# Gate columns in pairs by seven products of halves, w_pg scaled once, and the stages around them re-interleaved

## The chip, the cores and the metric

The kernel runs on all 8 cores of one Trainium2 chip, each with its own share of the batch and no traffic between cores. The metric is the device time of the slowest core, in microseconds (us). The engines are TensorE (PE in the rows), VectorE (DVE), ScalarE (ACT), GpSimd (POOL) and SyncE (SP); the last two issue most of the DMA transfers.

## The reference

One layer of a convolutional decoder trunk and a final norm, on 8 prompt sequences of 2048 tokens and 128 sample sequences of 8 tokens, width 1024. Per core that is one prompt sequence and 16 sample sequences: 2176 tokens.

```python
u = rmsnorm(h, g_mix)
proj = u @ w_in                        # (tokens, 9 * 1024)
a_b, a_c, a_h, a_z, b_v, b_g, b_z, gate_a, gate_b = split(proj)
s  = a_c * a_h                         # branch A
ya = (a_b * causal_dwconv(s, w_conv_a) * silu(a_z)) @ w_out_a          # 3 taps
v  = b_v * sigmoid(b_g)                # branch B
c  = causal_dwconv(v, w_conv_b) + b_conv_b                             # 31 taps
yb = (silu(layernorm(c, ln_g, ln_b)) * silu(b_z)) @ w_out_b
m  = sigmoid(gate_a) * ya + sigmoid(gate_b) * yb
h  = h + m @ w_o
h  = h + sigmoid(rmsnorm(h, g_ple) @ w_pg) * (p @ w_pe)
y  = rmsnorm(h, g_final)               # and the last rows of s and v, per sequence
```

## The kernel before

**Tiles.** A core's tokens go through in two blocks. Block 0 has 1152 tokens (9 tiles of 128) in two units of 2 x 288 tokens, block 1 has 1024 tokens (8 tiles) in one unit of 2 x 512. The normed, transposed input uT stays in SBUF as eight k tiles. Every projection is computed in chunks j = 0 to 7 of 128 output channels: weights of a chunk (128 x 1024, bf16) stay in the array's side and tokens stream, in `mm8` (L582), so a chunk of one column group takes 2 units x 2 halves x 8 k tiles = 32 products of 288 columns in block 0 and 16 of 512 in block 1.

**Weights.** 14 ring buffers of 256 KB are filled by GpSimd's queue (L394) in the order in which they are used (`WL`); a buffer that is done with lets the next transfer be issued.

**Order.** All operations are recorded by `S.add` in program order with what they read and write; an engine works in that order, and waits (semaphores) come from overlaps of reads and writes. There is no planner: the order in the code is the order on each engine. A block runs: the GLU projection, the 31-tap convolution (`s2_conv`, L720, on TensorE from re-laid-out copies R and Rs of prompt and sample rows, which SyncE loads at L687 and L694 from DRAM) and the short convolution chunk by chunk; then conv 6, gate and output product 0 of branch a (`s5_a`), conv 7, `s5_a(1)`, `ln_stats`, `s5_a(2)`, the z branch with LayerNorm applied (`s4_chunk`, z_j) mixed with `s5_a(3)` and `s5_a(4)`, `s5_a(5)` to `s5_a(7)`, and eight `s5_b` in the order 7, 0, 1, ... 6. Then the last stage, per tile: product with w_o (L1004), the residual (VectorE L1015) and its bf16 copy (ScalarE L1020), a transpose by DMA (L1024), products with w_pe (L1052) and w_pg (L1060), and the final norm and output. In block 0 the next block's first stage (statistics, `s1_scale`, transposes) is interleaved with that.

**Around the convolutions.** VectorE evacuates a convolution (L744, L748, a shuffle L751) and adds it and its square into accs and accq (L767, L771), in two parts each. `ln_stats` sums those over partitions by products with ones (L782), makes mean and variance (ScalarE L790, L792, VectorE L794), Ln and Exp (L797, L799), and sends both to DRAM and back, broadcast, into accs and accq (SyncE L803, L809). z's units wait for these (VectorE L923, L925), and ScalarE applies two silus (L918 on z, L927 on the norm).

**Gates.** `s5_half` runs a gate's chunk (columns 7 or 8 of w_in), its Tanh on ScalarE (L938), the output product of the same chunk and an evacuation on VectorE that multiplies with the gate (L946); branch b adds both (L977).

**w_pg.** In the b stage of each block SyncE loads w_pg in f32 (`wpg_stage`, L516, 512 KB a transfer, two staging buffers), ScalarE scales it with g_ple into bf16 (`wpg_scale`, L520, eight times a block).

## Time and profile before

| | |
|---|---|
| median of 3 runs (range) | 862.86 us (861.85 to 863.13) |
| span of the profiled execution (core 4) | 861.8 us |
| spans of the eight cores | 855.7 (core 3) to 861.8 us |
| mean granted clock of the cores | 0.995 to 0.998 |
| TensorE busy | 837.3 us, 97% |
| VectorE busy | 478.1 us, 55% |
| ScalarE busy | 304.0 us, 35% |
| GpSimd busy | 216.1 us, 25% |
| chain that ended last | TensorE 86%, DMA 4%, VectorE 4%, ScalarE 3% |
| 16 DMA engines, 258 to 300 us | 93% busy, 161 GB/s |

The profiled execution's span is 1.06 us under the median of the runs. A row of a timeline has a start, a length, engine, line, operation, output and inputs, and in brackets how long the engine had been idle and what it had waited for. Matmul ends are modelled, so the pace of TensorE is read from start to start. A granted clock of 1 is 2.4 GHz; 0.5 is 1.2 GHz.

### The profile page before, as it was taken

The numbers are of one execution on the slowest core, as the hardware profiler recorded it, in microseconds if no ns is written. First come the engines' busy times: TensorE is split into PE (matmuls) and PEld (weight loads), VectorE is DVE, ScalarE is ACT, GpSimd is POOL, SyncE is SP. The second block draws the span as 40 slices with busy tenths as digits, with TensorE's granted clock in tenths as the row PEclk, the third lists the DMA queues.
The fourth block names the chain that finished last, engine by engine and source line by source line (L and its number), as shares of the span: only waits on it lengthen the run. The fifth ranks groups of instructions, "written<-read, shape, count | busy, mean of one in ns | idle before, by whom it ended". The sixth has DMA issues, their size and how long they took to land.

```text
span 861.8 us, 16560 instructions; the slowest of 8 cores (855.7 to 861.8 us)
## 1 busy us (share of the span) xinstructions
PE 837.3 (97%) x5746; PEld 498.3 (58%) x5790; DVE 478.1 (55%) x676; ACT 304.0 (35%) x426; POOL 216.1 (25%) x402
## 2 busy tenths in 40 slices
PE   7899999999999999999899999999999999999995
PEld 3677777777777777775344444444444444444442
DVE  3545576766856742344776244555566483234566
ACT  3212232322344531434565212222224342242554
POOL 3532332332312111122442222222221221000121
PEclk9999999999999999999999999999999999999998
DMA  9999999999969864799998998998987899353533
GB/s 242 163 195 184 198 157 162 162 170 162 153 100 208 117 98 74 161 232 152 220 274 213 157 154 124 148 146 130 147 140 121 171 167 168 52 159 61 142 100 108
DMA packets 88826, 133.44 MB, mean 155 GB/s; under 512 B 37272, under 2 KB 45736, under 8 KB 86696
## 3 DMA queue, kind: packets, MB, share of 16 engines
q0 software_dynamic: 33392, 57.72, 44.7%
q1 hardware_dynamic: 55208, 74.40, 39.6%
q8 instruction: 47, 0.77, 0.4%
q14 instruction: 35, 0.29, 0.1%
q10 hardware_dynamic: 144, 0.26, 0.1%
HBM read 169.26 MB, written 17.25 MB: 216 GB/s over the span
## 4 chain that ended last, share of the span: by engine, by line
PE 86%; DMA 4%; DVE 4%; ACT 3%; issue 2%; SPq 0%; POOL 0%; DVEq 0%; POOLq 0%; ACTq 0%
PE ps L582 72%; PE ps L1060 5%; PE ps L1004 5%; PE ps L720 3%; DMA t_xs<-x 2%; PE ps L1052 1%; DMA t_ring<-w_in 1%; ACT t_tmp L414 1%; DVE t_cbuf L1015 1%; ACT t_tmp L738 1%; DMA t_u2T<-t_xb 1%; ACT t_cbuf L1074 1%; DVE t_tmp L861 0%; ACT t_xb L1020 0%; DVE t_uT L559 0%
## 5 line engine op out<-in xcount | busy, mean ns | idle before, releaser
L582 PE MATMUL ps<-t_uT,t_ring 128*128 128x288 bf16 (+1 forms) x3429 | 536.9, 316 | 6.0 <-DVE t_uT L559 2.2
L582 PEld LDWEIGHTS ps<-t_uT,t_ring 128*128 128x128 bf16 x3456 | 336.1, 98 | 200.5 <-issue 10.2
L394 POOL DMA_DIRECT2D t_ring<-w_in x144 | 79.1, 550 | 300.5 <-PE ps L582 279.1
L938 ACT ACTIVATE t_tmp<-ps 128x576 f32<-128x576 f32 (+1 forms) x48 | 36.7, 771 | 107.5 <-PE ps L582 107.5
L946 DVE SCALAR_TENSOR_TENSOR t_tmp<-t_tmp,ps 128x576 f32<-128x576 f32 (+1 forms) x27 | 24.6, 910 | 86.1 <-PE ps L582 86.1
L1060 PE MATMUL ps<-t_reg,t_u2T 128*128 128x512 bf16 x267 | 62.7, 386 | 3.4 <-DMA t_u2T<-t_xb 2.6
L582 PE MATMUL ps<-t_yaT,t_ring 128*128 128x288 bf16 (+1 forms) x383 | 61.7, 317 | 0.1
L582 PE MATMUL ps<-t_cbuf,t_ring 128*128 128x288 bf16 (+1 forms) x382 | 61.5, 317 | 0.1
L1004 PE MATMUL ps<-t_cbuf,t_yaT 128*128 128x512 bf16 x267 | 60.7, 379 | 0.3
L905 DVE TENSOR_TENSOR t_tmp<-ps,t_tmp 128x576 f32<-128x576 f32 (+1 forms) x24 | 21.8, 912 | 60.0 <-PE ps L582 60.0
L644 DVE SCALAR_TENSOR_TENSOR t_vta<-t_tmp,ps 128x512 bf16<-128x512 f32 (+1 forms) x24 | 20.7, 863 | 58.2 <-ACT t_tmp L641 50.7
L414 ACT ACTIVATE t_tmp<-t_cbuf 128x1024 bf16<-128x1024 f32 x37 | 38.8, 1049 | 39.0 <-DVE t_cbuf L1085 37.3
L641 ACT ACTIVATE t_tmp<-ps 128x576 f32<-128x576 f32 (+1 forms) x24 | 18.6, 775 | 91.1 <-PE ps L582 91.1
L582 PEld LDWEIGHTS ps<-t_yaT,t_ring 128*128 128x128 bf16 x384 | 37.4, 98 | 21.9 <-issue 0.6
L582 PEld LDWEIGHTS ps<-t_cbuf,t_ring 128*128 128x128 bf16 x384 | 37.6, 98 | 21.4
L1060 PEld LDWEIGHTS ps<-t_reg,t_u2T 128*128 128x128 bf16 x272 | 26.7, 99 | 37.3 <-issue 7.4
L417 POOL TENSOR_SCALAR t_msq<-t_ssq 128x1 f32<-128x1 f32 x50 | 15.9, 319 | 122.3 <-ACT t_tmp L414 121.9
L1004 PEld LDWEIGHTS ps<-t_cbuf,t_yaT 128*128 128x128 bf16 x272 | 26.5, 98 | 32.0 <-issue 0.3
L903 ACT ACTIVATE t_tmp<-ps 128x576 f32<-128x576 f32 (+1 forms) x24 | 18.6, 776 | 69.4 <-PE ps L582 69.4
L891 ACT ACTIVATE t_tmp<-ps 128x576 f32<-128x576 f32 (+1 forms) x24 | 18.6, 776 | 58.6 <-PE ps L582 52.9
L422 POOL TENSOR_TENSOR t_rsd<-t_msq,t_mhalf 128x1 f32<-128x1 f32 x50 | 34.4, 688 | 8.0 <-POOL t_msq L417 0.9
L738 ACT ACTIVATE t_tmp<-ps,t_vecs 128x512 f32<-128x512 f32 (+1 forms) x24 | 15.7, 654 | 52.4 <-PE ps L720 45.9
(115 smaller groups left out, 804.1 us busy)
## 6 DMA issues: line engine op xcount, KB each, us to landing
t_ring<-w_in POOLq DMA_DIRECT2D x144, 256.0 KB, 6.9
t_xs<-x SPq DMA_DIRECT2D x30, 512.0 KB, 6.6
y<-t_cbuf SPq DMA_DIRECT2D x16, 512.0 KB, 3.8
t_reg<-vd SPq DMA_DIRECT2D x32, 132.0 KB, 5.5
t_reg<-vd SPq DMA_DIRECT2D x32, 131.9 KB, 5.9
t_reg<-vd SPq DMA_DIRECT2D x32, 131.9 KB, 6.8
t_reg<-vd SPq DMA_DIRECT2D x32, 131.9 KB, 7.6
t_ring<-w_cv POOLq DMA_DIRECT2D x16, 256.0 KB, 9.0
```

What stands on the lines that cost most here:

```text
L394: S.add("pool", lambda e, k=k, src=src: e.dma_start(out=ring[k][:, :], in_=src), writes=[f"ring{k}"], dma=f"ring{k}")
L414: S.add("act", lambda e, c=c: e.activation(out=junk.rearrange("p (h m) -> p h m", h=2), in_=src_ap, func=AF.Square, accum_out=ssq[:, c:c + ...
L422: S.add("pool", lambda e, c=c: e.tensor_tensor(out=rsd[:, c:c + 1], in0=msq[:, c:c + 1], in1=mhalf[:, 0:1], op=ALU.pow), reads=[f"msq{c}", ...
L582: S.add("pe", lambda e, k=k, si=si, c0=c0: e.matmul(ps[:, b + si, 0:wb], lhsT=ring[k_][:, 128 * k:128 * k + 128], rhs=src[:, k, c0:c0 + wb ...
L644: S.add("dve", lambda e, bv=bv, tg=tg, u=u: e.scalar_tensor_tensor(out=pph(vt[v], u), in0=pcols(two(tg)), scalar=1.0, in1=pcols(pp(bv)), o ...
L720: S.add("pe", lambda e, b=b, r=r, i=i, g=g, wc=wc, rhs=src[:, c0:c0 + w], w=w: e.matmul(ps[32 * g:32 * g + 32, b + r, 0:w], lhsT=ring[kc][ ...
L738: S.add("act", lambda e, out=out, cols=cols: e.activation(out=cols(ph(te)), in_=out[0], func=AF.Identity, scale=vcol(V_MA), bias=vcol(V_BC ...
L905: S.add("dve", lambda e: e.tensor_tensor(out=two(tz), in0=pp(bb), in1=two(tz), op=ALU.mult), reads=pres(bb) + [tzr], writes=[tzr])
L938: S.add("act", lambda e: e.activation(out=two(tg), in_=pp(bg), func=AF.Tanh, scale=0.5), reads=pres(bg), writes=[tgr])
L946: S.add("dve", lambda e: e.scalar_tensor_tensor(out=dst.rearrange("p (s n) -> p s n", s=2), in0=two(tg), scalar=1.0, in1=pp(b), op0=ALU.ad ...
L1004: S.add("pe", lambda e, h=h, k=k: e.matmul(ps[:, b + h, :], lhsT=yaT[:, k, 128 * ti:128 * ti + 128], rhs=wo_t[:, k, 512 * h:512 * h + 512] ...
L1060: S.add("pe", lambda e, h=h, k=k: e.matmul(ps[:, bg + h, :], lhsT=u2Ts[sl][:, k, :], rhs=wpg_t[:, k, 512 * h:512 * h + 512], start=(k == 0 ...
```

## The change

**Gates by seven products.** Two chunks (ja, jb) of a gate and the two halves of a block's tokens form a 2 x 2 problem: halves of k (four k tiles each), two chunks, two halves of tokens. `g_pair` computes it with seven products of halves (4 matmuls each) and sums, in the form of Winograd. Sums of inputs (`us_make`: 4 operations on VectorE a block over 128 x 2304 bf16 elements in block 0 and 128 x 2048 in block 1) and of weights (`g_weights`: 4 of 128 x 512 a pair) go ahead; sums of products are made by accumulating in a PSUM bank, by copies on ScalarE (L1031) and by adds on VectorE (L1037). Banks X, C and Y are PSUM banks 0 to 2, and all other products of these stages rotate through bank pairs 2 and 3. Between the products, `fill` puts four matmuls at a time of an output product or of z (`halves`, L1076), three times in each half of a pair in block 0 (two halves) and in block 1's one. Gates 0 and 1 of branch a are computed as before (`gate_plain`); pairs are (2, 3), (4, 5), (6, 7) of branch a and four of branch b.

**Order.** Between conv 6 and `ln_stats` stood the gates and output products 0 and 1; now gate 0, conv 7, gate 1 and half of output product 0. `us_make(2)` stands right ahead of conv 6's evacuation. z, output products and pairs follow in a new order, unit by unit.

**w_pg.** In block 0 `pg_in` loads w_pg (SyncE), `pg_mul(k)` scales it on ScalarE (L551; "scaling k") and SyncE writes it to DRAM (wpgd) and then issues `pg_in(k + 2)`. The scalings stand behind z and output units: 0, 1 and 2 behind z00, output 2 unit 0 and z10; 3 behind pair (4, 5); 4 behind output 3 unit 0; 5, 6 and 7 behind z30, output 3 unit 1 and z31. In both blocks' b stage `wpg_load` loads the scaled weights from DRAM.

**Buffers.** xs, xn, xb, u2T, the short convolution's rows and the sums of inputs share SBUF; w_pg, w_pe and p of the last stage lie elsewhere in the same region; the x tiles are loaded in another order (own 0 and 1 first), and the first two tiles of the next block are normed at the start of the last stage of block 0 and not in the b stage.

The diff, cut to its core:

```diff
-            s2_conv(6)
-            s5_a(0)
-            flush(pend_sums)
-            s2_conv(7)
-            flush(pend_sums)
-            s5_a(1)
-            ln_stats()
-            s5_a(2)
-            for j in range(NCH):
-                s4_chunk(j)
-                last_weights("wo", [j])
-                if j in AFTER:
-                    s5_a(AFTER[j])
+                us_make(2)
+                s2_conv(6)
+                gate_plain(0)
+                flush(pend_sums)
+                s2_conv(7)
+                flush(pend_sums)
+                gate_plain(1)
+                g_weights(7, 2, 3)
...
+                if not bi:
+                    pg_in(0)
+                    pg_in(1)
+                    pgk.extend(range(NCH))
+                queue(("a", 0))
+                for _ in range(2 * U):
+                    step()
+                ln_stats()
+                rest()
+                queue(("a", 1))
+                gates("a", 7, 2, 3)
+                g_weights(7, 4, 5)
+                rest()
+                for p in (("z", 0, 0), ("a", 2, 0), ("z", 0, 1), ("z", 1, 0), ("a", 2, 1)):
+                    queue(p)
+                    rest()
+                    if p[2] == 0:
+                        pg()
+                queue(*((("z", 1, 1), ("z", 2, 0)) if U == 2 else (("z", 2, 0), )))
+                gates("a", 7, 4, 5)
+                pg()
+                rest()
+                g_weights(7, 6, 7)
+                for p in (("a", 3, 0), ("z", 2, 1), ("z", 3, 0), ("a", 3, 1), ("z", 3, 1), ("z", 4, 0), ("z", 4, 1)):
+                    queue(p)
+                    rest()
+                    if p != ("z", 2, 1):
+                        pg()
+                while pgk:
+                    pg()
+                queue(("a", 4, 0), ("z", 5, 0)) if U == 2 else queue(("a", 4))
+                gates("a", 7, 6, 7)
...
+                for i, j in enumerate(BORDER):
+                    queue(("b", j))
+                    if i in (0, 2, 4):
+                        if i < 4:
+                            g_weights(8, BORDER[i + 4], BORDER[i + 5])
+                        gates("b", 8, BORDER[i + 2], BORDER[i + 3])
+                    rest()
...
+            def pg_mul(k):
+                S.add("act", lambda e: e.activation(out=pgo[k % 2], in_=pgs[k % 2], func=AF.Copy,
+                                                    scale=vcol(V_GPLE, k)),
+                      reads=[f"pgs{k % 2}", "vecs"], writes=[f"pgo{k % 2}"])
+                S.add("sp", lambda e: e.dma_start(out=wpgd[k], in_=pgo[k % 2]),
+                      reads=[f"pgo{k % 2}"], writes=[f"wpgd{k}"], dma=f"pgo{k % 2}")
+                if k + 2 < NCH:
+                    pg_in(k + 2)
...
+                        prod(X, A[:, 0:512], ra, ut(0, wb * s), r1, True)
+                        copy(pt(C), X, [f"ps{C}"])
+                        prod(Y, d[0], [rd[0]], su(0), ["us0"], True)
+                        copy(v22, Y, r22)
+                        fill()
+                        prod(X, d[1], [rd[1]], su(1), ["us1"], False)
+                        plus(pt(Y), [f"ps{Y}"])
+                        prod(C, A[:, 512:D], ra, ut(4, wb * s), r1, False)
+                        evac(*th(ga, 0, s), pt(C), [f"ps{C}"])
+                        fill()
+                        prod(X, B[:, 0:512], rb, su(3), ["us3"], False)
+                        copy(pt(C), X, [f"ps{C}", "gx"])
+                        plus(v22, r22)
+                        prod(Y, B[:, 512:D], rb, su(2), ["us2"], False)
+                        evac(*th(gb, 0, s), pt(Y), [f"ps{Y}"])
+                        fill()
+                        prod(C, d[2], [rd[2]], ut(4, hf + wb * s), r2, False)
+                        evac(*th(gb, 1, s), v22, [])
+                        evac(*th(ga, 1, s), pt(C), [f"ps{C}"])
...
-            XU.extend(nxt[0:2])
-            for i in range(len(own)):
+                XU.extend(own[0:2] + nxt[0:3])
+                for i in range(2, len(own)):
...
-            if nxt:
-                s1_xbar(0, 0)
                 s6_Aev(0, *s6_A(0))
                 got = s6_A(1)
                 s6_B(0)
                 s6_Aev(1, *got)
+                if nxt:
+                    s1_scale(*s1_stats(nxt[0]), 0)
+                    s1_xbar(0, 0)
+                    pre[1] = s1_stats(nxt[1])
```

**Order on TensorE, block 0, from conv 6 (the first L720 or L759 rows) to LayerNorm's ones-products (t_accs, t_accq).** Before:

```order
L720 MATMUL ps<-t_reg,t_ring 32x512 x32
L720 MATMUL ps<-t_reg,t_ring 32x64 x32
L582 MATMUL ps<-t_uT,t_ring 128x288 x32
L582 MATMUL ps<-t_yaT,t_ring 128x288 x32
L720 MATMUL ps<-t_reg,t_ring 32x512 x32
L720 MATMUL ps<-t_reg,t_ring 32x64 x32
L582 MATMUL ps<-t_uT,t_ring 128x288 x32
L582 MATMUL ps<-t_yaT,t_ring 128x288 x32
L782 MATMUL ps<-t_accs,t_onesf 32x288 x4
L782 MATMUL ps<-t_accq,t_onesf 32x288 x4
```

Now (L621 is a plain gate, L1076 the filler or an output product):

```order
L759 MATMUL ps<-t_reg,t_ring 32x512 x32
L759 MATMUL ps<-t_reg,t_ring 32x64 x32
L621 MATMUL ps<-t_uT,t_ring 128x288 x32
L759 MATMUL ps<-t_reg,t_ring 32x512 x32
L759 MATMUL ps<-t_reg,t_ring 32x64 x32
L621 MATMUL ps<-t_uT,t_ring 128x288 x32
L1076 MATMUL ps<-t_yaT,t_ring 128x288 x16
L821 MATMUL ps<-t_accs,t_onesf 32x288 x4
L821 MATMUL ps<-t_accq,t_onesf 32x288 x4
L1076 MATMUL ps<-t_yaT,t_ring 128x288 x16
L1020 MATMUL ps<-t_uT,t_ring 128x288 x4
L1020 MATMUL ps<-t_mis,t_vt 128x288 x4
```

The output products, rows on t_yaT, are gone from between the convolutions; 48 products less stand ahead of the ones-products.

**Order on ScalarE, block 0, ahead of a gate.** Before, the last z units' silus (L918, L927), the gates' Tanh (L938) and then the scalings of w_pg (L520) in the b stage:

```order
L918 ACTIVATE t_tmp<-ps 128x576
L927 ACTIVATE t_tmp<-t_tmp,t_vecs 128x576
L938 ACTIVATE t_tmp<-ps 128x576 x12
L520 ACTIVATE t_reg<-t_xn,t_vecs 128x1024
L520 ACTIVATE t_reg<-t_xb,t_vecs 128x1024
L938 ACTIVATE t_tmp<-ps 128x576 x2
L520 ACTIVATE t_reg<-t_xn,t_vecs 128x1024
```

Now, ahead of pair (6, 7): scalings 5, 6 and 7 (L551), the silus (L1101, L1109) of z31, z40 and z41, and the pair's first copies (L1031) and Tanh (L1067):

```order
L551 ACTIVATE t_mis<-t_reg,t_vecs 128x1024
L551 ACTIVATE t_xs<-t_reg,t_vecs 128x1024
L1101 ACTIVATE t_tmp<-ps 128x576
L1109 ACTIVATE t_tmp<-t_tmp,t_vecs 128x576
L551 ACTIVATE t_mis<-t_reg,t_vecs 128x1024
L1101 ACTIVATE t_tmp<-ps 128x576
L1109 ACTIVATE t_tmp<-t_tmp,t_vecs 128x576
L1101 ACTIVATE t_tmp<-ps 128x576
L1109 ACTIVATE t_tmp<-t_tmp,t_vecs 128x576
L1031 ACTIVATE ps<-ps 128x288
L1031 ACTIVATE t_tmp<-ps 128x288
L1067 ACTIVATE t_tmp<-ps 128x288
```

The pair's first copy stands behind three scalings of w_pg that stood in the b stage.

**Order on VectorE, block 0, in branch b.** Before, evacuations (L946) and adds (L977) alone:

```order
L946 SCALAR_TENSOR_TENSOR t_tmp<-t_tmp,ps 128x576 x4
L977 TENSOR_TENSOR t_yaT<-t_tmp 128x576 x2
L946 SCALAR_TENSOR_TENSOR t_tmp<-t_tmp,ps 128x576 x2
L977 TENSOR_TENSOR t_yaT<-t_reg,t_tmp 128x576 x2
L946 SCALAR_TENSOR_TENSOR t_tmp<-t_tmp,ps 128x576 x2
L977 TENSOR_TENSOR t_yaT<-t_reg,t_tmp 128x576 x2
```

Now, at the pair of the third step: weight subtracts (L997), adds out of bank X (L1037), and an output unit's evacuation and add (L1149, L1157):

```order
L997 TENSOR_TENSOR t_vt<-t_ring 128x512
L997 TENSOR_TENSOR t_vt<-t_ring,t_vt 128x512
L997 TENSOR_TENSOR t_ring<-t_ring 128x512
L997 TENSOR_TENSOR t_vt<-t_ring,t_vt 128x512
L1037 TENSOR_TENSOR ps<-ps,t_tmp 128x288
L1037 TENSOR_TENSOR t_tmp<-ps,t_tmp 128x288
L1149 SCALAR_TENSOR_TENSOR t_tmp<-t_tmp,ps 128x576
L1157 TENSOR_TENSOR t_yaT<-t_reg,t_tmp 128x576
L1037 TENSOR_TENSOR ps<-ps,t_tmp 128x288
L1037 TENSOR_TENSOR t_tmp<-ps,t_tmp 128x288
L1149 SCALAR_TENSOR_TENSOR t_tmp<-t_tmp,ps 128x576
L1157 TENSOR_TENSOR t_yaT<-t_reg,t_tmp 128x576
```

An evacuation and its add now stand ahead of an add that the third product into bank X waits for.

## Rows read from the trace of the kernel before

**Rows 1.** The page's first part: busy us, share, instructions

```profile
PE 837.3 (97%) x5746; PEld 498.3 (58%) x5790; DVE 478.1 (55%) x676; ACT 304.0 (35%) x426; POOL 216.1 (25%) x402
```

**Rows 2.** TensorE's timeline: start us, us, engine line op out<-in xcount

```profile
329.13 4.08 PE L582 MATMUL ps<-t_uT,t_ring 128*128 128x288 bf16 x32
333.05 4.08 PE L582 MATMUL ps<-t_cbuf,t_ring 128*128 128x288 bf16 x32
...
733.44 3.62 PE L582 MATMUL ps<-t_uT,t_ring 128*128 128x512 bf16 x16
736.89 3.62 PE L582 MATMUL ps<-t_cbuf,t_ring 128*128 128x512 bf16 x16
```

**Rows 3.** TensorE's timeline, block 0, conv 7 and LayerNorm's ones-products

```profile
238.94 2.17 PE L720 MATMUL ps<-t_reg,t_ring 128*32 128x512 bf16 x64
...
249.02 0.69 PE L782 MATMUL ps<-t_accs,t_onesf 128*32 128x288 f32 x8
```

**Rows 4.** VectorE's timeline, block 0: conv 6, conv 7, last sum

```profile
232.42 0.74 DVE L744 SCALAR_TENSOR_TENSOR t_cbuf<-ps,t_vecs,t_tmp 128x512 f32<-128x512 f32 x1
...
242.47 0.74 DVE L744 SCALAR_TENSOR_TENSOR t_cbuf<-ps,t_vecs,t_tmp 128x512 f32<-128x512 f32 x1
...
247.58 0.75 DVE L771 TENSOR_TENSOR t_accq<-t_accq,t_tmp 128x576 f32<-128x576 f32 x1
```

**Rows 5.** Timelines of VectorE and TensorE, block 1, the same place

```profile
649.50 0.74 DVE L744 SCALAR_TENSOR_TENSOR t_cbuf<-ps,t_vecs,t_tmp 128x512 f32<-128x512 f32 x1
...
658.30 0.75 DVE L744 SCALAR_TENSOR_TENSOR t_cbuf<-ps,t_vecs,t_tmp 128x512 f32<-128x512 f32 x1
...
662.26 0.68 DVE L771 TENSOR_TENSOR t_accq<-t_accq,t_tmp 128x512 f32<-128x512 f32 x1
...
663.36 0.64 PE L782 MATMUL ps<-t_accs,t_onesf 128*32 128x256 f32 x8
```

**Rows 6.** Line 694, conv 7's sample rows, issue and landing

```profile
L694 SPq DMA_DIRECT2D t_reg<-vsd x8: 308/372/372, 223.3 to 226.5; - x8
...
DMA to landing us min/median/max: 10.0/10.2/11.1
```

**Rows 7.** Timelines of TensorE, VectorE and ScalarE behind LayerNorm, block 0

```profile
250.13 4.09 PE L582 MATMUL ps<-t_uT,t_ring 128*128 128x288 bf16 x32
...
250.65 0.46 DVE L794 SCALAR_TENSOR_TENSOR t_tmp<-ps,t_tmp 128x288 f32<-128x288 f32 x1 [0.56 <-ACT t_tmp L792]
...
253.57 1.28 ACT L938 ACT_TABLE_LOAD   x1
...
265.59 0.87 ACT L927 ACTIVATE t_tmp<-t_tmp,t_vecs 128x576 f32<-128x576 f32 x1 [4.74 <-DVE t_tmp L925]
```

**Rows 8.** Groups by line and shape: xcount | busy us, mean ns

```profile
L927 ACT ACTIVATE t_tmp<-t_tmp,t_vecs 128x576 f32<-128x576 f32 x16 | 13.9, 867 | 14.6 <-DVE t_tmp L925 14.6
...
L918 ACT ACTIVATE t_tmp<-ps 128x576 f32<-128x576 f32 x16 | 10.2, 639 | 12.2 <-PE ps L582 12.0
L927 ACT ACTIVATE t_tmp<-t_tmp,t_vecs 128x1024 f32<-128x1024 f32 x8 | 9.9, 1238 | 12.3 <-DVE t_tmp L925 12.3
...
L520 ACT ACTIVATE t_reg<-t_xn,t_vecs 128x1024 bf16<-128x1024 f32 x8 | 9.1, 1140 | 2.4 <-DMA t_xn<-w_pg 2.4
...
L1039 DVE COPY t_u2T<-ps 128x512 bf16<-128x512 bf16 x4 | 1.7, 425 | 5.9 <-PE ps L1033 5.9
```

**Rows 9.** Line 516, loads of w_pg: all, then 340 to 380

```profile
DMA to landing us min/median/max: 3.2/6.5/14.0
...
DMA to landing us min/median/max: 6.1/6.8/9.9
```

**Rows 10.** Chain of waits (start us, us); a stretch's busy times, clock

```profile
404.19 6.39 DMA t_xs<-x
...
426.98 5.15 PE ps L1060 x16
...
426.00:432.00 6.00, 5.03 (x17) 2.03 (x18) 3.25 (x3) 2.70 (x5) 2.47 (x5) 0.72 0.97 288
```

1902 lines of the change are left out of this document (1034 added, 868 removed).

## The prediction

> **What bounds the kernel now.** I read the page's first part, then TensorE's timeline, then what the other engines do at the joints of the stages. TensorE is busy 97% of the span [rows 1]: a product that goes away is time that goes away, and a wait put before a product is time that comes back. Where products follow each other without a gap, 32 of 288 columns take 333.05 − 329.13 = 3.92 us, 0.1225 each, and 16 of 512 columns 736.89 − 733.44 = 3.45 us, 0.2158 each [rows 2]. The profiled span is 861.8 us and the median of the runs 862.86; I sum against the span and add 1.06.
>
> **The products that go.** Two gate columns took 64 products of 288 columns in block 0 and 32 of 512 in block 1. Seven products of halves instead of eight make that 56 and 28. Gates 0 and 1 of branch a stay plain, so there are 7 pairs a block: 7 x 8 x 0.1225 + 7 x 4 x 0.2158 = 6.86 + 6.04 = **−12.9 us**. All that follows asks how much of it is given back.
>
> **LayerNorm's sums come too early, +3.4.** Before, four groups of 32 products stand between conv 6 and LayerNorm's ones-products, beside conv 7; now gate 0, conv 7, gate 1 and half of output product 0. In block 0 the ones-products stand 48 products sooner, at 249.02 − 5.88 = 243.1, and conv 7 stands 32 sooner, at 238.94 − 3.92 = 235.0 [rows 3]. In that time VectorE has to evacuate conv 6, add its sums, evacuate conv 7 and add those. It is free for conv 6 at 232.42; conv 7's chain runs from 242.47 until its last sum (four of 0.67 from start to start) ends at 248.25, 5.78 us [rows 4], so an evacuation alone is 3.1. Ahead of it stands a subtract over 2304 bf16 elements, 1.35 (below). The last sum is ready at 232.42 + 1.35 + 3.1 + 2.7 + 5.78 = 245.35, and the ones-products end at 246.1 instead of 244.2: +1.9. In block 1 they could start at 663.36 − 24 x 0.2158 = 658.2 and end 1.1 later; VectorE is free at 649.50, the subtract takes 1.2, and the chain 662.94 − 658.30 = 4.64, of which four sums of 0.6 [rows 5]: 649.5 + 1.2 + 2.24 + 2.4 + 4.64 = 660.0, the end 660.7 instead of 659.3: +1.5 (rounded up). Conv 7's sample rows are issued up to 226.5 and land 10.0 to 11.1 us later [rows 6], 236.5 to 237.6, where their products come at 235.0 + 1.9. A wait of up to 0.7 there costs nothing, for VectorE is busy with conv 6 until 239.6.
>
> **The price of the subtracts.** The trace has no operation on two bf16 tensors in SBUF. The nearest rows are a copy of 512 bf16 elements, 425 ns [rows 8], and an f32 add of 512, 0.68 us [rows 5]. I take the first, which has the type; with a fixed part of 0.15 from the f32 rows (0.75 at 576, 0.68 at 512) that is 1.35 us for 2304 elements and 0.36 from start to start for 512. The f32 end is a rival.
>
> **Behind LayerNorm in block 0, +1.9.** Four weight subtracts of pair 2, 3 (1.45) and an output evacuation (0.67) stand on VectorE ahead of LayerNorm's variance. It started 250.65 − 250.13 = 0.52 after the ones-products' end [rows 7]; that would be 246.6, and is 247.5 now. So Exp, which ended 3.4 after that end, ends 4.3 after it. Only behind it can ScalarE copy the pair's first product out of bank X, in which the third product accumulates: it waits until 4.3 + 0.35 + 0.13 = 4.8 and stands 28 products behind, at 3.4: 1.4. A table load of 1.28 stood ahead of Tanh [rows 7]; ahead of the pair's first Tanh it makes the copy behind that 0.5 late. In block 1 a product is 0.2158 long, and nothing is late. By the Trainium skill (ScalarE: Activation LUTs, Table sets: the hidden batching unit) copy is in every table set, so the load can't come before the first copy, where it would cost 1.28 and not 0.5. No row of the trace before has a copy right behind Exp.
>
> **Silus ahead of a pair, +2.4.** Where a pair follows a part of z, its first copy stands behind two silus, and X is written again 12 products after the pair's start. Block 0, before the first b pair: 0.26 + 0.64 + 0.87 + 0.41 + 0.13 = 2.3 against 1.5 [rows 8]: 0.8 (0.41 for a copy of 288 is an estimate from the row of 576; 0.26 and 0.13, for the hand-over from TensorE and back to it, are estimates too, of the size of the gap of 0.52 [rows 7], which holds one of each and more). Block 1, three times: 0.26 + 1.0 (0.64 scaled to 1024 columns) + 1.24 + 0.6 + 0.13 = 3.2 against 2.6: 0.6. Starts on ScalarE overlap by 0.08: −0.2.
>
> **Pairs of branch b in block 0, +2.9.** VectorE adds out of X before X is written a third time. The add can start 16 products + 0.26 = 2.2 after the start of a half of the pair, takes 0.46 [rows 7], and X is wanted at 24 products, 2.9: 0.1 to spare. In each of three pairs one output unit ends just ahead of it, whose evacuation and add (0.67 each) stand before it on VectorE: 3 x 0.7. One pair has four weight subtracts behind such an add: 0.8.
>
> **The embedding gate's weights, +7.1, and the clock, +1.5.** Scaling them took 16 x 1.14 us of ScalarE in the b stages [rows 8], hidden beside TensorE; that this goes is worth nothing. Now eight scalings stand among block 0's z and gate units, and scaling k needs transfer k, which SyncE issues only behind scaling k − 2. I take a landing of 6.5 us, the median of all [rows 9]. Scaling 0 stands behind the first unit's second silu, which started 265.59 − 250.13 = 15.5 after LayerNorm's end [rows 7] and 16.4 now, and ends at 264.5; transfer 2 is issued at 265.2 and lands at 271.7; scaling 2 ends at 272.85, the copy behind it at 273.3. Pair 4, 5's third product is wanted 196 products behind the ones-products, plus 1.9 of waits: 246.1 + 24.0 + 1.9 = 272.0. 1.3 late. From there, in the same way: scaling 3 ends 283.6, transfer 5 lands 290.8, scaling 5 ends 292.0, transfer 7 lands 299.2, scaling 7 ends 300.3, four silus until 303.1, the copy 303.6; pair 6, 7's third product is wanted 200 products after 273.3, at 297.8. 5.8 late. The bounds are wide: the shortest landing is 3.2, the longest 14.0, and 6.1 to 9.9 while the gates' weights stream [rows 9]. After a wait the clock can fall: before, 2.63 us of waiting at 426.98 are followed by 16 products in 5.15 us, where the clean pace is 3.45, at a mean granted clock of 0.72 [rows 10], so partly at the lower of the two levels. I take +1.5 once.
>
> **Last stage of block 0, −2.5.** The third own x tile was waited for 6.39 us at 404.19 [rows 10], since its load was issued behind the scale of a tile of the next block and two transposes. It moves some 3 us ahead, but the statistics and scale of a next tile now stand on ScalarE and VectorE there. I take 0.8, 0.2 of a smaller wait, and 1.5 of clock, which stays up if 2.63 becomes 1.8. Bounds: 0 and −4.
>
> **Sum.** −12.9 + 3.4 + 1.9 + 2.4 + 2.9 + 7.1 + 1.5 − 2.5 = +3.8: span 865.6, median **866.7 us**. Chance 0.34, its own range 864.6 to 871.
>
> **Rivals.** (1) Transfers land in 4 us or less. Pair 4, 5 is on time, pair 6, 7 waits 2.9, the clock stays: −12.9 + 3.4 + 1.9 + 2.4 + 2.9 + 2.9 − 2.5 = −1.9, **861.0**, and at 3.2 us 860.2. For it: one landing of 3.2; against it: the rows of 6.1 to 9.9. 0.22. (2) The short waits are covered, but 1.9 at one LayerNorm and 2 elsewhere: −9.0, **853.9**. For it: each was found from slack of under a microsecond, and a product that waits once gives slack to the next. Against it: VectorE's chain before LayerNorm has whole operations in it. 0.14. (3) Slower: the transfers take 12 us, as the two behind LayerNorm did, since lnd's broadcasts and output weights share the queues there. Each late step passes on: 6.8 + 11.3 instead of 7.1, **877.7**; the kernel is as fast as before at a landing of some 4.7 us and slower from there. 0.10. (4) Subtracts run at the f32 rate, 2.5 us for 2304 and 0.68 for 512: LayerNorm +2.3, behind it +1.0, b pairs +1.0, **871.0**. 0.12. By the Trainium skill (VectorE: DVE Perf Modes, The perf-mode tier table (the rule you actually need)) operations on two bf16 tensors in SBUF run at twice the f32 rate, which speaks against it; no run so far shows one. (5) The terms meet near 862.9: 0.08.
>
> **How the numbers follow.** The range reaches from the middle of rival 2 to just under rival 3, 855 to 876. A measurement of this kernel can tell about 0.2% from no change, 861.1 to 864.6. Faster: rival 2 and most of rival 1, 0.32. Same: the rest of rival 1, rival 5 and the low end of mine, 0.18. Slower: 0.50.
>
> **What to look for.** The ones-products wait for VectorE, 1.9 and 1.5. In block 0 two copies of bank X start right behind a scaling of w_pg that waited for its transfer; if the products behind them don't wait, that term falls. A subtract of 512 lasts 0.43 us, not 0.68. The wait at 426.98 is under 2 us. I am wrong if TensorE's added waits in the gate stages sum to under 10 or over 22 us.

## The result and the profile after

The changed kernel takes **890.0 us** (median of 4 runs), the kernel before beside it 863.0. The ratio is **1.0298, 95% interval 1.0273 to 1.0323**. Forecast were 866.7 and a range of 855 to 876: the sign was right, the size was not, and the range did not hold it. Ratios leave out runs in which one die's clock was down; medians hold them, so where the two disagree (f2 and f4, two such runs left in each) the ratio is given alone.

The page's first part, busy us, share and count, answers to [rows 1]:

```profile
PE 838.1 (94%) x5706; PEld 491.4 (55%) x5706; DVE 530.4 (60%) x782; ACT 331.0 (37%) x523; POOL 212.3 (24%) x402
```

TensorE is as long busy as before, though 12.9 us of products are gone, and its share fell from 97% to 94%: some products run slower, and the rest is waiting. The list of its waits says for what (line and what it waited for, us in total, times, longest). In it L1020 is a product of a pair, L1076 one of a filler, of z or of an output, L759 conv 7, and L1272 the product with w_pg:

```profile
PE ps L1076 <- ACT t_tmp L1101: 9.7, 1, 9.7
PE ps L1020 <- ACT ps L1031: 6.3, 7, 2.3
PE ps L1020 <- DVE ps L1037: 3.9, 5, 1.4
PE ps L1020 <- DVE t_reg L1149: 3.8, 1, 3.8
PE ps L759 <- DMA t_reg<-vsd: 3.8, 1, 3.8
...
PE ps L1272 <- DMA t_reg<-wpgd: 2.3, 1, 2.3
PE ps L1272 <- DVE t_cbuf L1227: 2.1, 1, 2.1
```

The longest, in its place: a z tile's banks are free only when its silu has run, and that stands behind scalings 5 and 6, which wait for their transfers. First ScalarE's timeline, then TensorE's (start, length, ..., in brackets the idle time before and what ended it):

```profile
304.51 1.15 ACT L551 ACTIVATE t_mis<-t_reg,t_vecs 128x1024 bf16<-128x1024 f32 x1 [6.43 <-DMA t_reg<-w_pg]
309.65 1.15 ACT L551 ACTIVATE t_xs<-t_reg,t_vecs 128x1024 bf16<-128x1024 f32 x1 [3.99 <-DMA t_reg<-w_pg]
310.70 0.63 ACT L1101 ACTIVATE t_tmp<-ps 128x576 f32<-128x576 f32 x1
```

```profile
311.48 4.00 PE L1076 MATMUL ps<-t_uT,t_ring 128*128 128x288 bf16 x16 [9.71 <-ACT t_tmp L1101]
```

The transfers of w_pg (line 547, the six issued between 270.7 and 306.1; the two before them took 3.3 and 4.6) took

```profile
DMA to landing us min/median/max: 3.8/7.3/16.1
```

and the 16.1 belongs to the transfer issued at 293.5, which scaling 6 waits for; the one issued at 291.1, for scaling 5, took 13.2. On the eight cores the longest took 14.2 to 16.1. The shortest, the median and the longest of all in the kernel before were 3.2, 6.5 and 14.0 [rows 9]; here the longest ones are the ones waited for. The Trainium skill (SBUF — State Buffer, The DMA setup-cost knee) has a fixed part of about 2 us and 436 GB/s behind it, from which 3.2 us is an estimate for these 512 KB. The trace agrees with that at its shortest, 3.3, and not at all where it counts. Six ring buffers and a piece of w_o were issued on GpSimd's queue between 287.1 and 295.0, just ahead of or beside the two slow transfers; that they are what slowed them was not tested.

The 16 products behind the wait take 4.00 us instead of 2.12. Three stretches of 7 to 8 us, around the stall of 2.35 us at 279.02 and the one of 9.71 at 311.48, have a granted clock of 0.57 to 0.76 (the number ahead of the DMA share), between the two levels, so the lower one is mixed in:

```profile
278.00:285.00 7.00, 5.98 (x37) 4.27 (x38) 2.04 (x4) 3.40 (x9) 0.02 (x1) 0.76 0.47 149
305.00:312.00 7.00, 0.53 (x3) 0.38 (x4) 0.00 (x0) 3.01 (x4) 0.00 (x0) 0.57 0.95 248
312.00:320.00 8.00, 7.98 (x49) 5.45 (x48) 3.41 (x5) 5.22 (x10) 0.53 (x1) 0.73 0.41 93
```

Conv 7 and the sums of LayerNorm, which answer to [rows 3]:

```profile
239.12 4.03 PE L759 MATMUL ps<-t_reg,t_ring 128*32 128x512 bf16 x64 [3.80 <-DMA t_reg<-vsd]
243.09 4.82 PE L621 MATMUL ps<-t_uT,t_ring 128*128 128x288 bf16 x32
247.74 2.12 PE L1076 MATMUL ps<-t_yaT,t_ring 128*128 128x288 bf16 x16
249.79 0.69 PE L821 MATMUL ps<-t_accs,t_onesf 128*32 128x288 f32 x8
```

From start to start conv 7 takes 3.97 here and 2.15 before, and the gate behind it 4.65 for 3.92: 2.6 us are lost to the clock behind this wait (0.50 from 239 to 243, 0.60 from 243 to 245). Block 1, TensorE, then VectorE, where a wait stands that the prediction does not know:

```profile
685.18 0.64 PE L821 MATMUL ps<-t_accs,t_onesf 128*32 128x256 f32 x8 [0.62 <-DVE t_accs L806]
...
691.95 1.86 PE L1020 MATMUL ps<-t_uT,t_ring 128*128 128x512 bf16 x4 [3.81 <-DVE t_reg L1149]
```

```profile
690.09 0.42 DVE L841 TENSOR_TENSOR t_tmp<-t_tmp 128x256 f32<-128x256 f32 x1 [2.49 <-ACT t_tmp L839]
690.47 1.22 DVE L1149 SCALAR_TENSOR_TENSOR t_reg<-t_xs,ps 128x1024 f32<-128x1024 f32 x1
```

Output product 0 lies in banks 0 and 1, which the first pair needs as X and C. Its evacuation (L1149) stands on VectorE behind LayerNorm's product of mean and deviation (L841), and that one waits for Exp.

The account, all from this trace against that of before (waits without the slow clock behind them; the clock apart, from start to start against the pace of [rows 2]):

| step of the prediction | forecast | measured |
|---|---|---|
| products | −12.9 | −12.9 by count |
| LayerNorm's sums, both blocks | +3.4 | 0.6, but 3.8 + 0.4 for conv 7's rows |
| behind LayerNorm, block 0 | +1.9 | 0.54 + 0.51 = 1.1 |
| silus ahead of a pair | +2.4 | 1.8 + 0.3 + 0.3 + 0.5 = 2.9 |
| pairs of branch b | +2.9 | 3.9 |
| w_pg's scalings | +7.1 | 2.35 + 9.71 = 12.1 |
| slow clock in the gate stages | +1.5 | 2.6 + 1.5 + 2.3 in block 0, 1.6 in block 1: 8.0 |
| last stage of block 0 | −2.5 | waits 2.3 + 2.1 against 2.6 before, clock 1.7 against 1.5: +2.0 |
| output product 0 behind Exp, block 1 | none | 3.8 |
| sum | +3.8 | +25.7 |

The spans differ by 889.5 − 861.8 = 27.7, so 2.0 us are left. They are of the size of what the idle times leave out: an idle time counts from the modelled end of the product before it, and from start to start a wait costs about 0.16 more. The four products at 367.21 take 0.49 at the pace, the idle time behind them is 0.77, and the next start is at 368.64, 1.43 later. The gate stages have 17 such waits now.

The prediction named a sign of its own for being wrong, added waits in the gate stages of under 10 or over 22 us. They are 28.6, the sum of the wait rows of this table without the last stage.

### The profile page after: what moved, and what is told of

The parts are those of the page before. It is cut to its first block, busy times and chain, and to the rows that moved or that the text cites. A ratio compares the mean times of both kernels' runs of the same rounds, so it can differ in the third digit from the quotient of the medians.

```text
span 889.5 us, 16897 instructions; the slowest of 8 cores (882.3 to 889.5 us)
## 1 busy us (share of the span) xinstructions
PE 838.1 (94%) x5706; PEld 491.4 (55%) x5706; DVE 530.4 (60%) x782; ACT 331.0 (37%) x523; POOL 212.3 (24%) x402
## 4 chain that ended last, share of the span: by engine, by line
PE 71%; DMA 9%; DVE 9%; issue 5%; ACT 3%; SPq 1%; POOL 1%; DVEq 0%; POOLq 0%; ACTq 0%
PE ps L621 36%; PE ps L1076 13%; PE ps L1020 9%; PE ps L1272 5%; PE ps L1216 4%; PE ps L759 3%; DMA t_reg<-w_pg 3%; DMA t_reg<-wpgd 2%; DMA t_xs<-x 2%; DMA t_reg<-vsd 1%; PE ps L1264 1%; DVE t_tmp L1104 1%; DMA t_ring<-w_in 1%; DVE t_cbuf L1115 1%; DMA vd<-t_vt 1%
## 5 line engine op out<-in xcount | busy, mean ns | idle before, releaser
L621 PE MATMUL ps<-t_uT,t_ring 128*128 128x288 bf16 (+1 forms) x2400 | 374.0, 317 | 3.5 <-DVE t_uT L598 2.3
L621 PEld LDWEIGHTS ps<-t_uT,t_ring 128*128 128x128 bf16 x2400 | 233.2, 98 | 141.2 <-issue 9.1
L1076 PE MATMUL ps<-t_uT,t_ring 128*128 128x288 bf16 (+1 forms) x384 | 65.3, 325 | 9.7 <-ACT t_tmp L1101 9.7
L1272 PE MATMUL ps<-t_reg,t_mis 128*128 128x512 bf16 x272 | 63.3, 386 | 4.9 <-DMA t_reg<-wpgd 2.3
L1076 PE MATMUL ps<-t_yaT,t_ring 128*128 128x288 bf16 (+1 forms) x384 | 65.7, 317 | 0.0
L1076 PE MATMUL ps<-t_cbuf,t_ring 128*128 128x288 bf16 (+1 forms) x384 | 64.4, 317 | 0.0
L946 DVE TENSOR_TENSOR t_tmp<-ps,t_tmp 128x576 f32<-128x576 f32 (+1 forms) x24 | 21.8, 912 | 60.1 <-PE ps L621 60.1
L1076 PEld LDWEIGHTS ps<-t_uT,t_ring 128*128 128x128 bf16 x384 | 38.5, 100 | 32.5 <-issue 10.0
L683 DVE SCALAR_TENSOR_TENSOR t_vt<-t_tmp,ps 128x512 bf16<-128x512 f32 (+1 forms) x24 | 20.7, 863 | 56.2 <-ACT t_tmp L680 40.7
L680 ACT ACTIVATE t_tmp<-ps 128x576 f32<-128x576 f32 (+1 forms) x24 | 18.6, 775 | 91.5 <-PE ps L621 91.5
L1076 PEld LDWEIGHTS ps<-t_yaT,t_ring 128*128 128x128 bf16 x384 | 37.4, 98 | 22.3 <-issue 1.4
L1076 PEld LDWEIGHTS ps<-t_cbuf,t_ring 128*128 128x128 bf16 x384 | 37.6, 98 | 21.4
L1272 PEld LDWEIGHTS ps<-t_reg,t_mis 128*128 128x128 bf16 x272 | 26.8, 99 | 39.1 <-issue 9.6
L944 ACT ACTIVATE t_tmp<-ps 128x576 f32<-128x576 f32 (+1 forms) x24 | 18.6, 776 | 68.9 <-PE ps L621 68.9
L1031 ACT ACTIVATE ps<-ps 128x288 f32<-128x288 f32 (+1 forms) x42 | 19.2, 457 | 62.4 <-PE ps L1020 61.3
L1149 DVE SCALAR_TENSOR_TENSOR t_tmp<-t_tmp,ps 128x576 f32<-128x576 f32 (+1 forms) x27 | 24.6, 910 | 28.0 <-PE ps L1076 28.0
L932 ACT ACTIVATE t_tmp<-ps 128x576 f32<-128x576 f32 (+1 forms) x24 | 18.6, 776 | 58.7 <-PE ps L621 49.8
```

Source lines behind the costliest of these rows:

```text
L621: S.add("pe", lambda e, k=k, si=si, c0=c0: e.matmul(ps[:, b + si, 0:wb], lhsT=ring[k_][:, 128 * k:128 * k + 128], rhs=src[:, k, c0:c0 + wb ...
L683: S.add("dve", lambda e, bv=bv, tg=tg, u=u: e.scalar_tensor_tensor(out=pph(vt[v], u), in0=pcols(two(tg)), scalar=1.0, in1=pcols(pp(bv)), o ...
L946: S.add("dve", lambda e: e.tensor_tensor(out=two(tz), in0=pp(bb), in1=two(tz), op=ALU.mult), reads=pres(bb) + [tzr], writes=[tzr])
L1031: S.add("act", lambda e: e.activation(out=out, in_=pt(b), func=AF.Copy), reads=[f"ps{b}"], writes=w)
L1076: S.add("pe", lambda e, k=k, si=si, c0=c0: e.matmul(ps[:, b + si, 0:wb], lhsT=ring[k_][:, 128 * k:128 * k + 128], rhs=src[:, k, c0:c0 + wb ...
L1149: S.add("dve", lambda e: e.scalar_tensor_tensor(out=dst.rearrange("p (s n) -> p s n", s=2), in0=two(o), scalar=1.0, in1=pp(b), op0=ALU.add ...
```

## The experiments

**Theory A**: the time is in transfers and chains of fixed length (w_pg in, wpgd out, the sample rows, Ln and Exp) that now stand on TensorE's path, each with a stretch of slow clock behind it. **Theory B**: it is the seven-product form itself, with its copies, additions and thin chains through one bank.

### One part away at a time

**e1_one_scaling.** Only rows 0 to 127 of w_pg are read, scaled and written out; the last stage reads them eight times.

```diff
-                if k + 2 < NCH:
-                    pg_in(k + 2)
...
-                    pg_in(1)
-                    pgk.extend(range(NCH))
+                    pgk.extend([0])
```

> The changed kernel (890.0 us) with only the first of the eight scalings of w_pg among z and gates; the other seven, their transfers in and their writes out are left out, and the last stages load the first scaled tile eight times (so the embedding gate's weights are not all there). Theory: scalings on ScalarE wait for transfers of w_pg that are issued two scalings before and queue behind a burst of ring weights; this stalls TensorE by 2.4 and 9.7 us in block 0, and each stall is followed by 1.4 to 2.3 us lost to a lower granted clock, and makes the copy ahead of the first b pair late (1.8). Without them: 890.0 - 16.5 = 873.5 us, ScalarE's idle time on w_pg gone. Rival: the silus and the pairs' own copies would keep ScalarE late anyway; then waits of 5 us or more stay in the same places and the time is 879 us or more.

Measured: 875.0 us, ratio 1.0141 (1.0117 to 1.0164), 0.0157 or 13.5 us below the changed kernel, near the 873.5 expected and not the rival's 879. The scalings of rows 1 to 7 are half of the loss. Left in its trace are 5.8 for the sample rows, 4.8 for copies behind silus, 3.7 behind Exp and 3.5 for additions.

**e2_no_rows7.** Conv 7's sample rows are not loaded (it works on the rows of an earlier chunk).

> The changed kernel without the loads of the sample rows (Rs) of chunk 7 in block 0, so that conv 7 uses the rows of chunk 5 for the sample tokens. Theory: the transfers' landing is what conv 7, moved 32 products ahead, waits for (3.8 us, and 2.6 more at a lower clock behind it); without them conv 7 runs at once, and then LayerNorm's ones-products wait some 1.9 us for VectorE's sums, which the stall hid: 890.0 - 4.5 = 885.5 us. Rival: the prompt rows, issued just ahead on the same queue, land as late, or VectorE's chain holds the end whatever TensorE does: 888.5 to 890.5 us.

Measured: 888.3, ratio 1.0293 (1.0266 to 1.0319): no different from the changed kernel; 885.5 was expected. The wait goes, and the one that the prediction had there comes out, at 1.73 for the forecast 1.9:

```profile
234.48 2.17 PE L759 MATMUL ps<-t_reg,t_ring 128*32 128x512 bf16 x64
244.40 0.69 PE L821 MATMUL ps<-t_accs,t_onesf 128*32 128x288 f32 x8 [1.73 <-DVE t_accs L806]
...
250.46 0.65 PE L1020 MATMUL ps<-t_mis,t_vt 128*128 128x288 bf16 x4 [1.27 <-ACT ps L1031]
```

TensorE is 5.4 us ahead at the sums. It is 4.4 ahead at the start of block 0's last stage (411.87 for 416.26), 3.1 at block 1's sums and 2.0 at the end; the profiled runs show that much, the ratios nothing. The transfers of w_pg are issued behind scalings and move with them (the long wait is 9.36 here), so they take nothing back. The last stage takes back 1.3, with 3.33 for a transposed tile and slow clock behind it, and block 1 another 1.1: behind the same wait of 3.81 as before the clock costs 2.7 here and 1.6 in the changed kernel.

**e3_bank_block1.** Output product 0 of block 1 and LayerNorm's sums go to banks 4 to 7 (`if U == 1: pairs[:] = [2, 3]`).

> The changed kernel, where in block 1 output product 0 and LayerNorm's ones-products take PSUM bank pairs 2 and 3 and not the ones that the first pair's banks X, C, Y lie in. Theory: the first product into X waits 3.8 us only because output product 0 lies in the same bank and its evacuation stands on VectorE behind LayerNorm's last operation, which waits for Ln and Exp; with other banks the pair starts at once, the first filler waits about 2 us for that evacuation instead, and the clock falls less: 887 us (886 to 888.5). Rival: the LayerNorm chain on ScalarE holds the pair as long whatever the bank: 889.5 to 890.5.

Measured: 884.1, ratio 1.0253 (1.0214 to 1.0292), some 4 us less where 3 were expected, with intervals that overlap, so its size is not shown. A wait behind the same evacuation remains, 2.08 in place of 3.81, at the next product that needs a bank.

**e4_eight_products.** Every pair as eight plain products in the new order, without subtracts, sums, copies and additions.

```diff
+                        for b, k_, g, h in ((0, ka, ga, 0), (1, kb, gb, 0), (2, ka, ga, 1), (0, kb, gb, 1)):
+                            prod(b, k_, hf * h + wb * s, (b, h) != (0, 1))
+                            evac(*th(g, h, s), ps[:, b, 0:wb], [f"ps{b}"])
```

> The changed kernel in its new order, with its fillers, its w_pg and its buffers, but every pair computed by plain products again (eight products of halves instead of seven, no weight or input subtracts, no copies or adds between banks). Theory: TensorE gets 12.9 us more of products and loses the waits of the seven-product form itself, which I put at 3.9 (adds out of X in branch b), 1.9 (copies in branch a's first pair and before the first b pair) and 1.0 in block 1: 890.0 + 12.9 - 7 = 896 us. Rival: the form's own waits and the clock behind them give back all it saves: 890 us or less.

Measured: 889.5, ratio 1.0309 (1.0288 to 1.0330), against 1.0298. The theory's 896 was a miss, the rival's 890 or less came out: in this order the seven products are worth some 1 us of 12.9, which the intervals do not tell from nothing. The starts of stages say where the rest is. Block 0's last stage starts at 412.40 here and at 416.26 in the changed kernel: in block 0 the eight products are the faster ones. They wait 7.66 at the scalings for 9.71, not at all for 2.35 + 1.4, 1.83 and 3.9, and 0.65 seven times for Tanh. From block 1's sums to the end the changed kernel takes 204.3 us and this one 209.8, 5.5 of the 6.04 in the count. So in block 0, with short products and scalings, B holds beside A: the form's own waits and the longer ones at the scalings take more than it saves. In block 1 it pays nearly in full.

### The same work in a better place

**f1_four_staging.** w_pg is read by GpSimd in bf16 into four buffers instead of two in f32, and the scalings stand further apart.

```diff
+        pgs = [regb[:, 8 * NTB + D * i:8 * NTB + D * (i + 1)] for i in range(4)]
...
+                if k + 4 < NCH:
+                    pg_in(k + 4)
```

> The changed kernel with all of its work, but w_pg comes in as bf16 through GpSimd's queue into four staging buffers instead of f32 through SyncE's into two, transfer k is issued behind scaling k - 4, and the scalings stand further apart (two ahead of z00, then behind z00, output 2 unit 0, pair 4-5, output 3 unit 0, z30 and output 3 unit 1). Theory: the distance between issue and use is what stalled ScalarE; with 16 us or more of distance the waits on w_pg go, as where they were left out: 876 us (874 to 878). Rival: the transfers, in the queue of the ring's weights, hold those up instead, and TensorE waits 3 us or more on ring buffers, or ScalarE is late by its own work: 880 or more.

Measured: 883.4, ratio 1.0242 (1.0210 to 1.0275), 7 us above the 876 expected. The loads are in time now, though which of queue, type, buffers and places did it can't be told from this run. ScalarE waits instead for write-outs, since two scalings later the same output buffer is needed:

```profile
  DMA wpgd<-t_xs: 7.1, 2
  DMA wpgd<-t_mis: 2.1, 2
```

(its idle time ahead of L552, us and times).

**f2_and_small_waits** adds to f1: banks as in e3, silus kept away from pairs, an output step ahead of each b pair, subtracts behind the pair.

> f1_four_staging and four reorderings: in block 1 output product 0 and LayerNorm's products in bank pairs 2 and 3; pairs follow an output product and not a z unit (both blocks); one filler step ahead of the b pairs of block 0, so that an output unit ends behind the add out of X and not ahead of it; weight subtracts of the next pair behind the pair. Theory: each wait has its own local cause, and the sum falls by what they measured: 5.9 (bank, as measured alone), 3.9 (adds in the b pairs), 1.8 + 1.0 (copies behind silus): 876 - 12 = 864 us. Rival: TensorE, earlier everywhere, meets what takes a fixed time (transfers of x, transposes, w_pg's reload) and half of it comes back there: 869 or more.

Measured: ratio 1.0127 (1.0085 to 1.0169), 10 us below f1. The additions' wait (3.5 in f1) is gone from its list, the copies' is down from 5.3 to 1.1. So these terms were real, at about their forecast size with some clock; 864 was missed by the write-outs, still 6.8, and by 5.3 for the sample rows.

**f3_and_conv7_later** puts output product 0 of block 0 ahead of conv 7.

```diff
+                if U == 2:
+                    queue(("a", 0))
+                    rest()
                 s2_conv(7)
```

> f2_and_small_waits, and in block 0 output product 0 stands between gate 0 and conv 7 as before the change, LayerNorm's ones-products stand behind half of output product 1, and the first pair has only four of its six fillers. Theory: conv 7 is back at the place where its rows have landed, so 3.8 us of waiting and 2.6 of slow clock go; the missing fillers cost 0.7, and LayerNorm waits about 1 for VectorE: f2's time less 5, about 859 us, faster than the kernel before. Rival: VectorE's chain of sums holds LayerNorm as it did when conv 7's rows were left out: f2's time less 1.5 or so.

Measured: 873.2, ratio 1.0122 (1.0087 to 1.0157), no different from f2, and 859 was expected. Conv 7's wait is gone, and block 0's sums stand at 247.6 for 251.3 in f2; but 2.5 of these 3.7 us go at the next write-out, where TensorE waits 7.08 for 4.61 (ScalarE, then TensorE):

```profile
274.71 1.15 ACT L552 ACTIVATE t_xs<-t_reg,t_vecs 128x1024 bf16<-128x1024 bf16 x1 [6.88 <-DMA wpgd<-t_xs]
```

```profile
278.49 4.00 PE L1077 MATMUL ps<-t_yaT,t_ring 128*128 128x288 bf16 x16 [7.08 <-ACT t_tmp L1102]
```

**f4_f3_eight_products** is f3 with the pairs as in e4.

> f3_and_conv7_later with plain gates, eight products of halves instead of seven, in the same order with the same fillers. Theory: where no transfer is waited for, seven products are worth the 12.9 us of products less some 2 of waits of the form's own (copies and adds): f3 + 11, about 870 us. Rival: the form's own waits and what they do to the clock give back most of it also here, as the comparison in the stalled kernel showed (889.5 against 890.0): f3 + 4 or less.

Measured: ratio 1.0243 (1.0209 to 1.0277): the seven products are worth 0.0121, 10.4 us, here, near the 11 expected.

**f5_rearranged** scales w_pg in place in four buffers outside the gates' region, puts pair 2, 3 ahead of LayerNorm's statistics and more products between it and the next pair; **f6_f5_eight** is f5 with eight products.

> All of the changed kernel's work, in a third order: w_pg comes as bf16 into four buffers outside the gates' region, is scaled in place and written out from there, scalings k and k+4 stand 25 us or more apart; pair 2-3 stands ahead of LayerNorm (fillers: output product 1), its weight subtracts in VectorE's gap ahead of conv 7's evacuation, 40 products stand between LayerNorm and the next pair; block 0 has output product 0 ahead of conv 7; no pair follows a z unit. Theory: of f3_and_conv7_later's 873 us (by its ratio to the kernel before), 7.1 us of waiting for a scaling whose output buffer was still being written to DRAM and 2.6 of slow clock behind it go, 2.5 and 1.5 at the first copy behind Exp, 1.1 of small waits in z, and about 4 at LayerNorm and the first pair of block 1: 858 us (856 to 861), faster than the kernel before. Rival: other fixed times take the place (the broadcast of LayerNorm's results, ring weights, x loads of the last stage): 864 or more.

> f5_rearranged with eight products of halves instead of seven. Theory: with the waits on transfers gone, the seven-product form is worth its 12.9 us of products less about 1.5 of its own waits: f5 + 11.5, near 870 us. Rival: as in the two comparisons so far (0 and about 10 us) some transfer or chain of fixed length still takes part of the saving: f5 + 8 or less.

Measured: f5 879.3, ratio 1.0211 (1.0190 to 1.0232); f6 896.5, ratio 1.0391. f5 was a miss by 21 us. ScalarE waits 7.73 for a load of w_pg again, and output products now stand right behind LayerNorm's waiting step:

```profile
333.12 1.15 ACT L550 ACTIVATE t_xs<-t_xs,t_vecs 128x1024 bf16<-128x1024 bf16 x1 [7.73 <-DMA t_xs<-w_pg]
```

```profile
265.52 5.75 PE L1074 MATMUL ps<-t_yaT,t_ring 128*128 128x288 bf16 x32 [3.85 <-DVE t_reg L1147]
```

The load was issued only at 317.4, behind the z unit where this order has it, and took 15.6 us, the longest of the eight; seven ring buffers had been issued between 308.6 and 314.3. The last write-out of its buffer had been issued at 287.8 and had landed 5.7 us later, so that was not what held it. That the two kinds of wait return, in other places, when the order around them changes is A's mark. f6 stands 15.5 us above f5, more than the 11.5 expected and than the 12.9 of the products. Its longest wait is 9.7 where f5's is 8.2, and seven waits for Tanh within the pairs, 4.7 in all, are its own; the account is not closed further.

### The write-outs, and what is left then

**g1_f3_four_outputs** is f3 with four output buffers for the scaled rows. **g2_f3_one_scaling** is f3 with the seven other scalings and their transfers left out, as in e1.

```diff
-        pgo = [t[:, 12 * HMAX:12 * HMAX + D] for t in (xsa.bitcast(BF16), mis)]
+        pgo = [t[:, a:a + D] for t, a in ((xsa.bitcast(BF16), 12 * HMAX), (mis, 12 * HMAX),
+                                          (xsa.bitcast(BF16), 8 * HMAX), (xsa.bitcast(BF16), 8 * HMAX + D))]
```

> As f3_and_conv7_later (873.2 us, ratio 1.0122), but the scaled rows of the gate weights have four buffers on the chip instead of two, so that a scaling does not wait until the rows of two scalings earlier have reached DRAM; in return the gates keep fewer temporaries in block 0. In the trace of f3, ScalarE waits 6.88 us ahead of a scaling for such a write-out, TensorE then 7.08 us for a silu behind it, and the slow clock after it takes 2.6 more. Theory (the write-out's landing is what costs): these 9.7 us go, about 864 (861 to 867). Rival (the silus are late in any case, by the landing of the next rows or by the scalings' own time): the wait comes back under another name, 870 to 874.

> As f3_and_conv7_later, but only the first of the eight row groups of the gate weights is read, scaled and written out; the last stage reads the scaled group eight times, so the seven others are left out of the computation and of the transfers. All products, their order and the waits of the steps stay. Theory (in this order the scalings are what keeps the seven products from paying): the 9.7 us go and seven scalings of 1.14 us no longer stand ahead of silus, so 861 to 863, level with the kernel before, and no more, since 2.5 + 1.5 us behind LayerNorm and 3.3 us in block 1 remain. Rival (transfers of w_pg slow the other DMAs and stages too): well below, 856 to 859.

Measured: g1 863.5 us, ratio **1.0018 (0.9998 to 1.0037)**; g2 863.6, 1.0016 (1.0002 to 1.0030). Both as A had it, both level with the kernel before. g1 is 9.0 us below f3 by one pair of buffers, and since g2 is no faster, all of the seven scalings' price in this order was waiting: their 7 x 1.14 us of ScalarE and their traffic cost nothing that a measurement can tell. The long waits in g1's gate stages are down to

```profile
PE ps L1078 <- DVE t_reg L1151: 2.6, 2, 2.1
PE ps L1022 <- ACT ps L1033: 2.5, 1, 2.5
```

and some of 1.2 or less. Both are LayerNorm's: a copy, and an output evacuation, behind a step that waits for Exp.

**g3_ln_split** records LayerNorm in three pieces, so that nothing waits behind Ln and Exp: the sums; Ln and Exp behind the pair's first two copies; L846 and the deliveries one or two output steps later. **g4_g3_eight** is g3 with eight products.

```diff
+                def fill_ln():
+                    if len(parts) == 2:
+                        parts.pop(0)()
+                        step()
+                    else:
+                        step()
+                        if parts:
+                            parts.pop(0)()
...
+                gates("a", 7, 2, 3, fill_ln)
```

> As g1_f3_four_outputs (863.5 us, ratio 1.0018), but LayerNorm's statistics are recorded in three pieces: the sums and VectorE's subtraction as before; Ln and Exp behind the first two copies of the next pair of gates; VectorE's product of mean and deviation, with the write-out and the four reads behind it, one step of output product later. In block 1 the whole of output product 0 stands ahead of the sums. In g1's trace the copy behind Exp costs TensorE 2.46 us at 256.39 in block 0 with 1.5 of slow clock; in block 1 the sums wait 1.19 and the output product behind the waiting VectorE step 2.08, with some 1.5 of clock. Theory (these named waits are what still takes the products' gain): 8 to 9 us less, 854 to 856, the first version faster than the kernel before. Rival (gone elsewhere): the delivery of the statistics, one to two us later, makes the first z tiles late, and 860 to 863 remain.

> As g3_ln_split with the merge gates in eight products per pair (plain products of whole rows, no subtractions, no sums of halves). By the counts eight products are 12.9 us more TensorE work. Theory (with the waits gone the seven products give nearly all of it): 10 to 13 us above g3. Rival (their short waits, copies and additions eat half or more): 3 to 7 us above g3.

Measured: g3 864.6 us, ratio 1.0011 (0.9994 to 1.0029); g4 871.5, ratio 1.0113 (1.0092 to 1.0135). For g3 854 to 856 was expected, and the rival's 860 to 863 is nearer. The named waits went (1.54 is left of 2.46, with no slow clock; none of them in block 1, where 1.08 for a silu and 1.02 for a copy are new), and the time of the slowest core did not. The spans of the profiled run say where it is, here of five of its cores:

```profile
core 3: 851.0 us, clock 0.998
core 4: 861.7 us, clock 0.993
core 5: 853.3 us, clock 0.996
core 6: 856.6 us, clock 0.994
core 7: 864.6 us, clock 0.994
```

Over the runs that the ratios use, the mean core takes 855.5 us in g3 and 858.1 before, the slowest 862.2 and 860.9, the fastest 850.9 and 855.9. So g3 gains 2.6 us on the mean core and 5 on the fastest, and the measure, the slowest, sees none of it. Seven products against eight are worth 11.7 us on the mean core and 8.8 by the ratios, under the 10 to 13 expected. The cores differ in the delivery of LayerNorm's statistics from DRAM. Here core 3, then core 7 (issues by queue, KB each, median us to landing):

```profile
t_accs<-lnd SPq DMA_DIRECT2D x2, 288.0 KB, 4.1
t_accq<-lnd SPq DMA_DIRECT2D x2, 288.0 KB, 4.6
```

```profile
t_accs<-lnd SPq DMA_DIRECT2D x2, 288.0 KB, 8.0
t_accq<-lnd SPq DMA_DIRECT2D x2, 288.0 KB, 11.2
```

and on core 7 TensorE then waits 2.51, 0.68, 1.79 and 1.31 at 272 to 282. In block 0 these reads land after 6.7 to 9.0 us on all cores of the kernel before (medians by queue), 3.7 to 5.9 in g1 and 3.7 to 11.2 in g3, so the spread came with g3.

**g5_a2_first**: output product 2 ahead of z tile 0. **g6_w_pg_later**: besides, the first transfers of w_pg behind the first pair. **g7_pair_first**: besides, pair 4, 5 with output product 3 ahead of the z tiles.

> As g3_ln_split, but output product 2 stands ahead of z tile 0 (in block 0 half by half), so that TensorE has 3.9 to 4.2 us more work, and VectorE an evacuation more, ahead of the first step that needs LayerNorm's statistics; the product of mean and deviation is recorded ahead of the second output step instead of behind it. Theory (late statistics make the slow cores slow): VectorE's waits for the statistics (2.8 and 6.5 us on core 7) no longer stand ahead of a1's and a2's evacuation, cores 4 and 7 come down to the 851 to 858 of the others, and the slowest core to 857 to 860 in all. Rival (a spread of the cores that is not this wait): 863 to 865 as g3.

> As g5_a2_first, but the first four transfers of w_pg are issued behind the first pair of gates, so behind LayerNorm's statistics, and the scalings stand later by about three steps. In g5's trace the reads of the statistics land after 4 to 5 us on core 0 and 8 to 11 us on cores 5 and 6, whose copy waits 6.5 and 4.0 us. Theory (the w_pg transfers, 9 to 12 us each and issued 10 us ahead, hold the statistics up): the reads land after about 4 to 6 us on all cores, the slow cores come down by 4 to 7, 857 to 860 in all. Rival (the ring's weights and the other cores do it): landings of 8 to 11 us remain on some core, 863 to 865.

> As g6_w_pg_later, but the second pair of gates with output product 3 stands ahead of the z tiles, so that some 19 us of TensorE work instead of 4 lie between the statistics and the first step that needs them. Theory (only the statistics' lateness makes the cores differ): all cores like the fast ones, 851 to 856 on each core, 856 to 859 for the slowest, faster than the kernel before by 0.4 to 0.7%. Rival (another transfer, a scaling or a fence is late next): as g6 or above, with another wait at its head.

| | median us | ratio (95%) | mean core | slowest | fastest |
|---|---|---|---|---|---|
| before, beside g6 and g7 | 862.5 | | 857.9 | 860.3 | 855.6 |
| g3 | 864.6 | 1.0011 (0.9994 to 1.0029) | 855.5 | 862.2 | 850.9 |
| g5 | 864.4 | 1.0003 (0.9979 to 1.0027) | 856.0 | 862.0 | 851.6 |
| g6 | 864.6 | 1.0030 (1.0015 to 1.0044) | 858.4 | 863.0 | 854.1 |
| g7 | 862.6 | 1.0003 (0.9991 to 1.0016) | 857.6 | 860.7 | 854.8 |

(The last three columns are means of the cores' spans over the runs that the ratios use.) g5 missed its 857 to 860: the statistics' wait left the evacuations and showed on ScalarE, whose silu of z stands ahead of the next pair's copies:

```profile
277.12 0.87 ACT L1116 ACTIVATE t_xs<-t_xs,t_vecs 128x576 f32<-128x576 f32 x1 [5.56 <-DVE t_xs L1114]
```

```profile
280.63 1.12 PE L1027 MATMUL ps<-t_mis,t_vt 128*128 128x288 bf16 x4 [6.48 <-ACT ps L1038]
```

(core 5). In g6 block 0's statistics landed after 3.6 to 7.1 us on all cores, 5.2 and 5.6 on the profiled one, about as expected, but there the copies wait 7.1 in all in four places, 2.08 and 1.33 of it where a scaling now stands right ahead of a pair's first copy (275.13 and 304.24); its 857 to 860 was a miss too. g7 brought the cores as close together as before (854.8 to 860.7), at their mean of before: its theory held for the spread and failed for the level, 862.6 where 856 to 859 was expected. Its waits are in the last stage of block 0 now, on core 7 2.95 for the residual sum of an x tile (DVE L1234) and 2.46 for a transposed tile. No version here beats the kernel before by more than a measurement can tell.

## Why the prediction was wrong, and where it was right

**Sign and method.** "All that follows asks how much of it is given back" was right, and the answer was more than all. The small terms were right in kind and within 1 us in size, but for LayerNorm's sums: subtracts of 512 at 422 ns and of 2304 at 1350 [rows 8 gave the estimate; with the fixed part of 0.15 it is 1.39, not 1.35], which rules out rival 4; silus ahead of pairs 2.9 for 2.4; additions 3.9 for 2.9; behind LayerNorm 1.1 for 1.9; the sums 0.6 for 3.4, since conv 7 was late itself, and 1.73 where e2 took that away. By the Trainium skill (ScalarE: Activation LUTs, Table sets: the hidden batching unit) the load could not come before the first copy; the rows agree, a copy right behind Exp and the load (1.28) only ahead of Tanh.

**The step that failed most: "I take a landing of 6.5 us, the median of all."** The transfers that mattered took 13.2 and 16.1. The 14.0 stood in [rows 9], and the row of 6.1 to 9.9 was no bound, as it shows a stretch with other traffic. The term was 12.1 and not 7.1, with 3.8 of clock behind its two stalls; e1 puts the whole at 13.5. Rival 3 had the mechanism, at 12 us and a chance of 0.10, and gave 877.7.

**"+1.5 once" for the clock.** The forecast had two stalls at the scalings and charged one. Behind the stalls of this trace TensorE lost 2.6 (wait 3.80), 1.5 (2.35), 2.3 (9.71) and 1.6 (3.81), 8.0 in the gate stages; behind the 1.83 at 342.17 and the 2.29 at 429.96 nothing. The 5.15 us of [rows 10] are a modelled length: the next product starts at 431.96, so 1.5 were lost there, which is what the prediction took.

**"A wait of up to 0.7 there costs nothing."** Conv 7's sample rows were last issued at 229.0 and not at 226.5, since their issue follows other work than before, and landed 8.1 to 9.7 later, so the wait was 3.8. That I took an issue time from the trace of before for a queue that the change reorders was the slip. By e2 it is worth 2.0 us at the end of the profiled runs, of 5.4 at its place, and nothing that the ratios tell.

**A wait that was not seen at all.** Output product 0 in block 1: 3.81 and 1.6 of clock. The prediction followed the DVE queue ahead of LayerNorm's variance, but not what stands behind a step that waits for Exp, and not which banks the pair takes over. "In block 1 a product is 0.2158 long, and nothing is late" was wrong there. In e3 the wait falls to 2.08 with other banks, and in g3, where nothing stands behind Exp, it is gone.

**The last stage, −2.5**, was +1.4 (77.7 us against 76.3, from start to start; its listed waits and clock alone make +2.0): the x tile's wait of before went as forecast (the 6.39 of [rows 10] are the transfer's own time in the chain, of which VectorE waited 3.08 at 410.75), and waits for wpgd (2.3) and for the residual sum of a later tile (DVE L1227, 2.1) took its place.

**The form of the sum.** The rest is not one step. The sum took 12.9 us of products as saved wherever they stood, and priced each wait of the form alone. But the value of the seven products followed from what stands around them: about 1 us in the changed order (e4, not told from nothing), 8.8 in g3's, 10.4 in f3's, 15.5 in f5's. One pair of buffers was worth 9 us (g1), and where a transfer of fixed length stood ahead, most of a gain of 3.7 us went there (f3).

**Open.** g4 does the product work of the kernel before and takes 1.13% more. Its list has 5.7 us of waits for Tanh at banks used twice within a pair; the rest, some 4 us, is not traced. Nor is it shown why one core's reads of the statistics land after 4 us and another's after 11; that w_pg's transfers play a part is only suggested by g6. They can't be all of it: in block 1, where w_pg is not read, the reads land after 4.0 to 5.2 us in g1 and 6.3 to 10.3 in g3.

## What to carry to other kernels

Count what is taken off the bottleneck only as far as the next thing that it waits for, a transfer already issued or a chain through DRAM and two engines. For a transfer placed on the path take the longest landing among bursts of other loads, not the median, and count its way out of the buffer as well as its way in: two more buffers were worth 9 us. Never record the evacuation of an accumulator behind an operation that waits for another engine's chain, and where the slowest of eight cores is the measure, look at all eight spans: a gain on the mean core can vanish in their spread.

## What the runs showed of the hardware that was not expected

- Loads of w_pg, 512 KB in f32, in the changed kernel: 3.3 to 16.1 us to landing; write-outs of 256 KB to DRAM 2.1 to 13.0, median 4.3.
- TensorE's clock after a wait: 0 to 2.7 us lost, and not in proportion to the wait (2.3 behind 9.71, 2.6 behind 3.80, 1.5 behind 2.35, 2.6 behind 7.08 in f3; behind the same 3.81 in block 1 1.6 in the changed kernel and 2.7 in e2). The 1.83 at 342.17 here and the 1.54 in g3 were followed by the full pace.
- Eight cores with the same program and no traffic between them: 5 us apart in the kernel before, 11 apart in g3, from run to run on other cores.
